# A two-layer decoder trunk on one core: SBUF residues of matmul operands, and the expert's last gate and up blocks as two 512-column slots

## The chip, the cores and the metric

The kernel runs on one core of a Trainium2 chip. The metric is the device time of one execution in microseconds. Before the change it is 1515.24 us, the median of 3 runs (1514.55 to 1516.45).

## The reference

Batch 1, 256 tokens, width 1024, two layers, all in float32. What matters here is which matrices are multiplied:

```python
for l in range(DEPTH):                      # 2 layers
    z = rms_norm(x, mix_norm[l]) @ w_in[l]  # 1024 x 5632: u 512 | q k v 1024 each | two gates 1024 each
    y_a = gelu(s5_branch(u, ...)); y_a = y_a * sigmoid(y_a @ w_glu[l] + b_glu[l])
    y_b = rms_norm(diff_attention(rope(q), rope(k), v, lam), subln[l]) * (1 - lam_init)
    m = sigmoid(g_ssm) * (y_a @ w_proj_ssm[l]) + sigmoid(g_attn) * (y_b @ w_proj_attn[l])
    x = x + m @ w_out[l]
    h = rms_norm(x, ffn_norm[l])
    # layer 0: dense (silu(h @ wg) * (h @ wu)) @ wd, inner width 2816
    # layer 1: the same for 8 experts, top 2 of them per token, weighted
    x = x + (swiglu(h, ...) if l == 0 else moe_swiglu(h, ...))
return rms_norm(x, final_norm)
```

## The kernel before

All weights come as a stream of slots of 128 x 2048 float32 (1 MB), 33 slots for each of three segments (layer 0's mixer, the dense feed-forward, layer 1's mixer) and 33 for each of eight expert rounds. SyncE loads a slot into `w_raw`. ScalarE rounds it into `w_hi` (L562) and VectorE writes the rest into `w_lo` (L568), both as float32r. Every product is then three matmuls (`mm3`, L1758 to L1760): hi x hi, lo (of the stationary operand) x hi, hi x lo (of the moving operand). TensorE's own split operands are `hT` (normed activations, transposed), `yS` and `yB` (the two branches), `actT` (dense activations), `hsT` (the rows of one expert), `eactT` (its activations), `y_slots` and `selectT` (the scatter of an expert's output).

There are two kinds of product. In the U block, the GLU, and the dense gate and up, the weights are stationary (128 x 128 pieces) and the activations move, 256 columns at a time: 48 matmuls a slot. Everywhere else the activations are stationary and the weights move, 512 columns at a time: 24 matmuls a slot in the mixers and in the dense down products (two token tiles), 12 in an expert round. The exception is the expert's last block: the inner width is 2816 = 5 x 512 + 256, so block 5 of gate and of up is 256 wide, one slot each (8 pieces of 256 columns, 24 matmuls).

Segment 1 (dense) runs g0 u0 and then g(j+1) u(j+1) d(j) for j = 0 to 9, then d10. Segments 0 to 2 use three split buffers, slot i in buffer i mod 3. An expert round uses five: three of `w_hi`/`w_lo` and two more, `w_hi_more0/1` and `w_lo_more0/1` (`ROUND_POS`). The splits of ScalarE and VectorE run two slots ahead of TensorE, three in a round. The order on every engine is written out by hand with semaphores; nothing plans it. SyncE also carries small transfers between its loads: twenty for the `s_direct` tile of layer 1 (`shift_direct`, L663) stand between the loads of slots 26 and 27 of segment 1.

The SBUF tiles are laid out one behind the other (`sb`, `room`). For the change the start addresses modulo 512 bytes matter. Slices of weights and activations step by multiples of 512 bytes (128 float32), so every slice of a tile has the tile's residue.

| tiles | residue before |
| --- | --- |
| `hT_hi`, `hT_lo`, `eactT_hi`, `eactT_lo` | 128 |
| `w_hi`, `w_lo`, every slot | 128 |
| `ident`, `identb` / `maskb` | 128 / 384 |
| `hsT`, `actT`, `yS`, `yB`, `y_slots`, `selectT`, `eact_tok`, `x_normed`, `w_hi_more`, `w_lo_more`, q, k, v and the S5 tables | 320 |

Of the kernel before, what the change touches and what calls it, by code (L numbers as in the profile page):

```python
# [9 lines left out]
F32R = mybir.dt.float32r  # L10
# [3 lines left out]
ALU = mybir.AluOpType  # L14
# [29 lines left out]
SLOT = 2048  # L44
SEG = 33
NRAW, NW, AHEAD = 4, 3, 2
RAW_POS = [i % 4 if i < 24 else (i - 24) % 3 for i in range(SEG)]
RAW_USES = [RAW_POS.count(p) for p in range(NRAW)]
GROUP_BLOCK = 512
# [52 lines left out]
ROUND_SLOTS += [("g", 1, 0), ("g", 1, 1), ("u", 1, 0), ("u", 1, 1)]  # L102
for _j in range(2, NB - 1):
    ROUND_SLOTS += [("g", _j, 0), ("d", 2 * _j - 4, 0), ("g", _j, 1), ("d", 2 * _j - 3, 0), ("u", _j, 0), ("u", _j, 1)]
ROUND_SLOTS += [("g", NB - 1, 0), ("u", NB - 1, 0)] + [("d", _m, 0) for _m in range(2 * NB - 6, NJ)]
ROUND_AT = {what: i for i, what in enumerate(ROUND_SLOTS)}
LAST_UP = [ROUND_AT["u", j, 1 if j < NB - 1 else 0] for j in range(NB)]
SCATTERS = [(0, 0, 6), (0, 1, 7), (1, 0, 0), (1, 1, 1)]
NR, RAHEAD = 5, 3
REST_AT, MID_AT, LO_AT = (9, 12), (15, 18), (18, 21)  # L110
# [79 lines left out]
def trunk(nc, t):  # L190
    ctx = ExitStack()
    with ctx:
# [11 lines left out]
        def sb(name, shape, dt=F32):  # L204
            a = here[0]
            here[0] += size(shape, dt)
            return at(name, shape, dt, a)
# [12 lines left out]
        hTh = at("hT_hi", [P, KD, SEQ], F32R, a_hT)  # L220
        hTl = at("hT_lo", [P, KD, SEQ], F32R, a_hT + 8192)
        raw = sb("w_raw", [P, NRAW, SLOT])
        wh = sb("w_hi", [P, NW, SLOT], F32R)
        wl = sb("w_lo", [P, NW, SLOT], F32R)
        ident = sb("ident", [P, P])
        identb = sb("identb", [P, P], BF16)
        maskb = sb("maskb", [P, P], BF16)
# [43 lines left out]
        U4 = sb("uT_lags", [P, PAIRS, BLK])  # L271


        a_q, a_k, a_v = room(8192), room(8192), room(8192)
        a_u, a_yh, a_yl = room(4096), room(4096), room(4096)
        a_tab = room(32768)
# [245 lines left out]
        def raw_of(seg, i):  # L522
            p = (RAW_POS if seg < 3 else ROUND_POS)[i]
            return raw[:, p, :] if p < NRAW else rawx[:, 0, :]

        def split_of(seg, i):

            p = i % NW if seg < 3 else ROUND_POS[i]
            if p < NW:
                return wh[:, p, :], wl[:, p, :]  # L530
            return whx[p - NW][:, 0, :], wlx[p - NW][:, 0, :]

        def landed(seg, i, r=None):
# [539 lines left out]
        def _(dve):  # L1073
# [604 lines left out]
            def dve_round(r, first):  # L1678

                own.r = r  # L1680
                his = [0]

                def hi_taken(name):

                    his[0] += 1
                    assert [w for w in ROUND_TR if w[:2] != "ST"][his[0] - 1] == name
                    dve.wait_ge(s_thi, r * NB + (THI0 + his[0]))
                    return TR0 + ROUND_TR.index(name)

                def act_lo(j):  # L1690
                    t, n = hi_taken(f"act{j}"), block_width(j)
                    V.tensor_tensor(bTl[:, j % 2, 0:n // P].rearrange("p k n -> p (k n)"), bank(4 + t % 2)[:, 0:n],
                                    bTh[:, j % 2, 0:n // P].rearrange("p k n -> p (k n)").bitcast(F32),
                                    ALU.subtract).then_inc(s_trf[t % 2], 1)

                for i in range(SEG):
                    if i == 3:
                        scattered(r)
                        for q in range(NT):
                            n = TR0 + ROUND_TR.index(f"ST{q}")  # L1700
                            dve.wait_ge(s_tr, r * R_TR + (n + 1))
                            V.tensor_copy(ST[:, q * P:(q + 1) * P], bank(4 + n % 2)[:, 0:P]).then_inc(s_trf[n % 2], 1)
                    if i in (29, 31):
                        act_lo(4 + (i - 29) // 2)
                    if i in (30, 31):
                        dve.wait_ge(s_hsh, r * 2 + (2 + i - 29))
                        hs_lo(i - 30)
                    round_split(dve_split, dve, i, r)
                    if first and i in REST_AT:
                        q = REST_AT.index(i)  # L1710
                        dve.wait_ge(s_hsw, 2)
                        dve.wait_ge(s_xh, q + 1)
                        V.tensor_tensor(xn[:, q, :], xn[:, q, :], xnh[:, q, :], ALU.subtract).then_inc(s_xr, 1)
                    if first and i in LO_AT:
                        q = LO_AT.index(i)
                        dve.wait_ge(s_xm, q + 1)
                        V.tensor_tensor(xnl[:, q, :], xn[:, q, :], xnm[:, q, :], ALU.subtract).then_inc(s_xl, 1)
                    if i == 4:
                        dve.wait_ge(s_scatv, r * 4 + 4)
                        own.do(V.tensor_copy(gcol[:, :], gateR[:, :, bass.ds(r, 1)].rearrange("p t o -> p (t o)")))  # L1720
                    if i in (7, 13, 19, 25):
                        act_lo((i - 7) // 6)
                    if i == SEG // 2:

                        own.do(V.tensor_copy(pcol[:, :], placeR[:, :, bass.ds(r + 1, 1)].rearrange("p t o -> p (t o)")))
                        select()
                    if i in LAST_UP[:5] or i == 28:
                        j = LAST_UP.index(i) if i in LAST_UP else 5
                        n = block_width(j)
                        dve.wait_ge(s_sg, r * NB + (GU0 + j + 1))  # L1730
                        if j == 5:
                            dve.wait_ge(s_tr, r * R_TR + (TR0 + ROUND_TR.index("act4") + 1))
                        V.tensor_tensor(moe_act[:, 0:n], moe_sg[:, 0:n], bank(3 + 4 * (j % 2))[:, 0:n], ALU.mult).then_inc(s_act, 1)

                for c in range(2):
                    dve.wait_ge(s_ysh, r * 2 + (c + 1))
                    V.tensor_tensor(ysl[:, c * 512:(c + 1) * 512], bank(c), ysh[:, c * 512:(c + 1) * 512].bitcast(F32),
                                    ALU.subtract).then_inc(s_ysl, 1)
# [14 lines left out]
        def _(pe):  # L1753
# [344 lines left out]
            with pe.Fori(0, rounds) as r:  # L2098

                def up(i):  # L2100

                    kind, j, h = ROUND_SLOTS[i]
                    n = block_width(j)
                    if kind == "g" and h == 0:
                        if j == 0:
                            pe.wait_ge(s_hsf, r * 2 + 1)
                        elif j == 1:
                            pe.wait_ge(s_scatv, r * 4 + 2)
                        else:
                            pe.wait_ge(s_act, r * NB + (GU0 + j - 1))  # L2110
# [3 lines left out]
                    nk = SLOT // n  # L2114
                    H, L = parts(3, i, nk)
                    for k in range(nk):
                        m = mm3(bank(2 + 4 * (j % 2) + "gu".index(kind))[:, 0:n], hsh[:, nk * h + k, :], hsl[:, nk * h + k, :],
                                H[:, k, :], L[:, k, :], start=(h == 0 and k == 0), stop=(nk * h + k == KD - 1))
                    m.then_inc(s_gu if i in LAST_UP else s_used, 1)

# [94 lines left out]
def round_slot(gate, up, down, what):  # L2215
    kind, j, h = what
    if kind == "d":
        return slot_of(down, 2 * j, 2, 0, D)
    n = block_width(j)
    return slot_of(gate if kind == "g" else up, SLOT // n * h, SLOT // n, 512 * j, n)  # L2220


def weight_stream(a):
# [41 lines left out]
```

## Time and profile before

| what | value |
| --- | --- |
| median of three runs | 1515.24 us |
| the profiled execution, first to last instruction (the only time the page has for it) | 1514.5 us |
| TensorE busy | 1475.5 us, 97%, 9071 matmuls |
| VectorE / ScalarE busy | 1226.9 us (81%) / 888.7 us (59%) |
| one expert round | 98.25 us, eight of them |
| 256-column products with `w_hi` or `w_lo` stationary and `hT` moving | 416 in each of L1758, L1759, L1760 |
| 512-column products with `hsT` stationary, `w` / `w_more` moving | 384 / 256 in each of the three lines |
| mean granted TensorE clock over the span | 0.993 |

TensorE takes a new matmul before the last one has ended, so a matmul's duration (0.28 us for 256 columns, about 0.39 for 512) is longer than the time from its start to the next start. The latter is what a stretch costs. It is read from the timeline: the difference of two start times, divided by the number of matmuls between them.

### The profile page before, as it was taken

To read this page: it belongs to the slowest core of one execution; us is meant where nothing else is said; L and a number is where in the kernel's file an instruction comes from. 1 tells how busy PE (TensorE), PEld (TensorE's weight loads), DVE (VectorE), ACT (ScalarE), POOL (GpSimd) and SP (SyncE) were. 2 spreads that over 40 slices of the span, in tenths; PEclk is the share of its full clock that TensorE was granted. 3 is DMA by queue.
4 is the path that set the end of the run, shared out by engine and by line. 5 is a ranking of instruction groups with operands and counts; after the bars stand their busy time and mean duration, and the time that the engine had idled before them with its cause. 6 is when DMAs were issued, how large, how long until landed. Compare 5 with 4: busy or idle time off the path is not lost.

```text
span 1514.5 us, 23848 instructions
## 1 busy us (share of the span) xinstructions
PE 1475.5 (97%) x9071; PEld 1247.5 (82%) x9071; DVE 1226.9 (81%) x1307; ACT 888.7 (59%) x887; POOL 74.1 (5%) x123
## 2 busy tenths in 40 slices
PE   7999999999999999998999999999999999999997
PEld 6788878999988888887888888888888888888886
DVE  7897786665456787867999989888888898988987
ACT  5244654443344346634677677767677767767775
POOL 2900100000000000101000000000000000000000
PEclk9899999999999999999999999999999999999999
DMA  6444444554355443353999989999999998998994
GB/s 247 156 139 149 151 154 180 209 175 180 92 204 198 167 150 108 142 197 146 366 360 347 378 335 353 359 345 361 346 346 370 341 357 339 350 374 334 351 360 166
DMA packets 76931, 393.09 MB, mean 260 GB/s; under 512 B 28225, under 2 KB 28353, under 8 KB 30018
## 3 DMA queue, kind: packets, MB, share of 16 engines
q1 hardware_dynamic: 75392, 391.28, 68.9%
q10 hardware_dynamic: 1474, 0.91, 0.2%
q8 instruction: 44, 0.72, 0.2%
q14 instruction: 21, 0.17, 0.0%
HBM read 388.36 MB, written 1.05 MB: 257 GB/s over the span
## 4 chain that ended last, share of the span: by engine, by line
PE 88%; DVE 6%; ACT 2%; issue 2%; SPq 1%; DMA 1%; POOL 0%; DVEq 0%; ACTq 0%; POOLq 0%
PE psum L1758 26%; PE psum L1760 26%; PE psum L1759 26%; PE psum L1774 3%; PE psum L2072 1%; DVE w_lo L568 1%; ACT w_hi L562 1%; SPq L663 1%; PE psum L1825 1%; PE psum L1870 1%; PE psum L2095 1%; PE psum L1807 1%; PE psum L2096 1%; PE psum L1800 0%; DMA w_raw<-in_stream 0%
## 5 line engine op out<-in xcount | busy, mean ns | idle before, releaser
L568 DVE TENSOR_TENSOR w_lo<-w_raw,w_hi 128x2048 fp32r<-128x2048 f32 x270 | 613.7, 2290 | 146.6 <-ACT w_hi L562 145.5
L562 ACT ACTIVATE w_hi<-w_raw 128x2048 fp32r<-128x2048 f32 x270 | 513.8, 1914 | 247.2 <-PE psum L1760 221.6
L1758 PE MATMUL psum<-w_hi,hsT_hi 128*128 128x512 f32 (+1 forms) x512 | 188.7, 369 | 2.1 <-issue 2.1
L1759 PE MATMUL psum<-w_hi,hsT_lo 128*128 128x512 f32 (+1 forms) x512 | 186.9, 365 | 0.0
L1760 PE MATMUL psum<-w_lo,hsT_hi 128*128 128x512 f32 (+1 forms) x512 | 186.7, 365 | 0.0
L1758 PE MATMUL psum<-w_hi,hT_hi 128*128 128x512 f32 x384 | 156.4, 407 | 4.8 <-DVE w_lo L568 4.6
L1760 PE MATMUL psum<-w_lo,hT_hi 128*128 128x512 f32 x384 | 151.3, 394 | 0.0
L1759 PE MATMUL psum<-w_hi,hT_lo 128*128 128x512 f32 x384 | 151.2, 394 | 0.0
L568 DVE TENSOR_TENSOR w_lo_more<-w_raw,w_hi_more 128x2048 fp32r<-128x2048 f32 x56 | 128.1, 2287 | 12.3 <-ACT w_hi_more L562 12.3
L1758 PE MATMUL psum<-hT_hi,w_hi 128*128 128x256 f32 x416 | 119.1, 286 | 4.9 <-DVE act_ff L1508 3.1
L1759 PE MATMUL psum<-hT_hi,w_lo 128*128 128x256 f32 x416 | 118.5, 285 | 0.0
L1760 PE MATMUL psum<-hT_lo,w_hi 128*128 128x256 f32 x416 | 118.4, 285 | 0.0
L562 ACT ACTIVATE w_hi_more<-w_raw 128x2048 fp32r<-128x2048 f32 x56 | 107.0, 1910 | 10.2 <-DMA w_raw<-in_stream 6.5
L1758 PEld LDWEIGHTS psum<-w_hi,hsT_hi 128*128 128x128 f32 x512 | 96.6, 189 | 18.2 <-issue 2.3
L1760 PEld LDWEIGHTS psum<-w_lo,hsT_hi 128*128 128x128 f32 x512 | 96.6, 189 | 16.8
L1759 PEld LDWEIGHTS psum<-w_hi,hsT_lo 128*128 128x128 f32 x512 | 96.7, 189 | 15.6
L1758 PE MATMUL psum<-w_hi_more,hsT_hi 128*128 128x512 f32 x256 | 102.4, 400 | 0.0
L1760 PE MATMUL psum<-w_lo_more,hsT_hi 128*128 128x512 f32 x256 | 100.2, 391 | 0.0
L1759 PE MATMUL psum<-w_hi_more,hsT_lo 128*128 128x512 f32 x256 | 99.6, 389 | 0.0
L1059 ACT ACTIVATE esilu_g<-psum 128x512 f32<-128x512 f32 (+1 forms) x48 | 27.1, 564 | 113.0 <-PE psum L1760 113.0
L568 DVE TENSOR_TENSOR w_lo_more<-w_raw_more,w_hi_more 128x2048 fp32r<-128x2048 f32 x40 | 91.4, 2284 | 0.1
L1758 PEld LDWEIGHTS psum<-w_hi,hT_hi 128*128 128x128 f32 x384 | 73.3, 191 | 20.5 <-DVE w_lo L568 5.2
(400 smaller groups left out, 2796.6 us busy)
## 6 DMA issues: line engine op xcount, KB each, us to landing
w_raw<-in_stream SPq DMA_DIRECT2D x326, 1024.0 KB, 5.6
w_raw_more<-in_stream SPq DMA_DIRECT2D x40, 1024.0 KB, 6.7
gain_row<-in_gain_rows SPq DMA_DIRECT2D x3, 512.0 KB
x_tok<-in_x SPq DMA_DIRECT2D x1, 1024.0 KB, 4.9
uT_lags<-uT_by_lag SPq DMA_DIRECT2D x64, 16.0 KB, 1.9
zT_by_lag<-uT_lags SPq DMA_DIRECT2D x64, 16.0 KB, 1.8
out_trunk<-out_tok SPq DMA_DIRECT2D x2, 512.0 KB, 2.6
s_direct<-s_direct_lags SPq DMA_DIRECT2D x40, 16.0 KB, 2.0
```

The source lines that it names most:

```text
L562: nc.scalar.activation(split_of(seg, i)[0], raw_of(seg, i), ACT.Copy).then_inc(s_hi, 1)
L568: nc.vector.tensor_tensor(l_, raw_of(seg, i), h.bitcast(F32), ALU.subtract).then_inc(s_lo, 1)
L663: sp.dma_start(Tm[rows(g, d), :, LAGS - 1 - d + e, :], TS[rows(g, e), :, :]).then_inc(s_tm, 16)
L1059: nc.scalar.activation(moe_sg[:, 0:n], bank(2 + 4 * (j % 2))[:, 0:n], ACT.Silu).then_inc(s_sg, 1)
L1758: mm(out, lh, rh, start=start, stop=False)
L1759: mm(out, ll, rh, start=False, stop=False)
L1760: return mm(out, lh, rl, start=False, stop=stop)
L1774: i = nc.tensor.transpose(dst[:, k * P:(k + 1) * P], s, ident[:, :])
L1807: mm(b[r, p * GCH:(p + 1) * GCH], Bl[l][r, c, p, :, :].rearrange("p d n -> p (d n)"), E[r, p, 0, :], start=(p == 0 and c == 0), stop=False)
L1825: mm(bank(2 + c)[:, off:off + n], qT[c * 64:(c + 1) * 64, h, q * P:(q + 1) * P], kT[c * 64:(c + 1) * 64, h, 0:n], start=(q == 1), stop=False)
L1870: i = mm(bank(6)[r, c * 256 + k * BLK:c * 256 + (k + 1) * BLK], Bt[r, c, p, :], U4[r, p, :], start=(k == 0 and c == 0), stop=(k == 3 and c ...
L2072: i = mm(bank(2 + g)[:, kk * P:(kk + 1) * P], part[:, q, k * P:(k + 1) * P], S[:, q, :], start=(part is xnh and kk == 0 and q == 0), stop= ...
```

## The change

Three things. First, padding: a pad after `w_hi` and one ahead of `a_q` bring `w_lo` and all the tiles from `a_q` on to the residue of `hT`, 128. Second, the three split buffers get 48 elements (192 bytes) at their end, and where a slot's weights are the stationary operand, the slot is put 192 bytes further, at residue 320. This holds for the dense gate and up slots (all but the first up slot, i = 1) and for the first slot of each mixer segment (the first half of the U block). The buffers are also renumbered, `(p + 2) % NW`. Third, the last gate and up blocks, 256 columns each, are laid side by side in the stream, so that the two slots are the upper and the lower half of the 1024 rows with 512 columns, gate in columns 0 to 255 and up in 256 to 511. Both accumulate in one bank, and VectorE takes up from its second half. The number of slots, their bytes and the waits stay.

```diff
+LEAD = 48
-ROUND_SLOTS += [("g", NB - 1, 0), ("u", NB - 1, 0)] + [("d", _m, 0) for _m in range(2 * NB - 6, NJ)]
+ROUND_SLOTS += [("gu", NB - 1, 0), ("gu", NB - 1, 1)] + [("d", _m, 0) for _m in range(2 * NB - 6, NJ)]
-LAST_UP = [ROUND_AT["u", j, 1 if j < NB - 1 else 0] for j in range(NB)]
+LAST_UP = [ROUND_AT["u" if j < NB - 1 else "gu", j, 1] for j in range(NB)]
...
-        wh = sb("w_hi", [P, NW, SLOT], F32R)
-        wl = sb("w_lo", [P, NW, SLOT], F32R)
+        wh = sb("w_hi", [P, NW * SLOT + LEAD], F32R)
+        here[0] += (a_hT - here[0]) % 512
+        wl = sb("w_lo", [P, NW * SLOT + LEAD], F32R)
...
+        here[0] += (a_hT - here[0]) % 512
         a_q, a_k, a_v = room(8192), room(8192), room(8192)
...
+        def stationary(seg, i):
+
+            if seg == 1:
+                return i % NW != 1 and FFN_SLOTS[i][0] != "d"
+            return seg != 3 and i == 0
+
         def split_of(seg, i):
 
             p = i % NW if seg < 3 else ROUND_POS[i]
             if p < NW:
-                return wh[:, p, :], wl[:, p, :]
+                a = (p + 2) % NW * SLOT + (LEAD if stationary(seg, i) else 0)
+                return wh[:, a:a + SLOT], wl[:, a:a + SLOT]
...
-                        V.tensor_tensor(moe_act[:, 0:n], moe_sg[:, 0:n], bank(3 + 4 * (j % 2))[:, 0:n], ALU.mult).then_inc(s_act, 1)
+                        ups = bank(3 + 4 * (j % 2)) if j < NB - 1 else bank(2 + 4 * (j % 2))[:, n:2 * n]
+                        V.tensor_tensor(moe_act[:, 0:n], moe_sg[:, 0:n], ups[:, 0:n], ALU.mult).then_inc(s_act, 1)
...
-                    n = block_width(j)
-                    if kind == "g" and h == 0:
+                    n = 512
+                    if kind[0] == "g" and h == 0:
...
-                        m = mm3(bank(2 + 4 * (j % 2) + "gu".index(kind))[:, 0:n], hsh[:, nk * h + k, :], hsl[:, nk * h + k, :],
+                        m = mm3(bank(2 + 4 * (j % 2) + (kind == "u"))[:, 0:n], hsh[:, nk * h + k, :], hsl[:, nk * h + k, :],
...
+    if kind == "gu":
+        last = np.concatenate([w[:, 512 * j:512 * j + block_width(j)] for w in (gate, up)], 1)
+        return slot_of(last, 4 * h, 4, 0, 512)
+    return slot_of(gate if kind == "g" else up, 4 * h, 4, 512 * j, 512)
```

The residues after it: 128 for `hT`, `eactT`, `hsT`, `actT`, `yS`, `yB`, `y_slots`, `selectT`, `eact_tok`, `x_normed`, both `w_more` pairs and every `w` slot whose weights move; 320 for the `w` slots with the lead and for `ident` and `identb`; 64 for `maskb`.

On TensorE the instructions change in one place, the last gate and up blocks of a round. Before, the end of the slot ahead, and the boundary from the gate slot to the up slot (`hsT` are the expert's rows, stationary; `act_ready` frees the banks):

```order
L1760 MATMUL psum<-w_lo,hsT_hi 128x512
L2113 REGISTER_ALU [waits act_ready]
L1758 MATMUL psum<-w_hi,hsT_hi 128x256 [waits w_lo_ready]
L1759 MATMUL psum<-w_hi,hsT_lo 128x256
L1760 MATMUL psum<-w_lo,hsT_hi 128x256
...
L1760 MATMUL psum<-w_lo,hsT_hi 128x256
L2113 REGISTER_ALU
L1758 MATMUL psum<-w_hi,hsT_hi 128x256 [waits w_lo_ready]
L1759 MATMUL psum<-w_hi,hsT_lo 128x256
```

The same place now, on TensorE again (line numbers of the changed kernel are 11 higher here):

```order
L1771 MATMUL psum<-w_lo,hsT_hi 128x512
L2124 REGISTER_ALU [waits act_ready]
L1769 MATMUL psum<-w_hi,hsT_hi 128x512 [waits w_lo_ready]
L1770 MATMUL psum<-w_hi,hsT_lo 128x512
L1771 MATMUL psum<-w_lo,hsT_hi 128x512
...
L1771 MATMUL psum<-w_lo,hsT_hi 128x512
L2124 REGISTER_ALU
L1769 MATMUL psum<-w_hi,hsT_hi 128x512 [waits w_lo_ready]
L1770 MATMUL psum<-w_hi,hsT_lo 128x512
```

Each of the two slots had 24 matmuls of 256 columns and has 12 of 512 now; the waits stand in the same places. ScalarE, VectorE, GpSimd and SyncE have the same instructions in the same order.

## Rows read from the trace of the kernel before

**Rows 1.** The page, shares of the chain that ended last.

```profile
PE 88%; DVE 6%; ACT 2%; issue 2%; SPq 1%; DMA 1%; POOL 0%; DVEq 0%; ACTq 0%; POOLq 0%
```

**Rows 2.** By stretch: length, busy PE PEld DVE ACT POOL, PEclk, DMA share, GB/s.

```profile
288.00:422.00 134.00, 132.73 (x1121) 123.53 (x1119) 78.94 (x81) 52.48 (x43) 0.00 (x0) 1.00 0.47 165
910.32:1008.57 98.25, 98.25 (x501) 81.55 (x500) 86.91 (x60) 69.48 (x49) 0.00 (x0) 1.00 0.92 353
```

**Rows 3.** SyncE queue's waits in one round, 910.32 to 1008.57: total, times, longest.

```profile
SPq L620 <- DVE w_lo L568: 54.6, 21, 5.4
SPq L620 <- DVE w_lo_more L568: 22.8, 11, 4.7
```

**Rows 4.** Timeline of TensorE (start us, duration us, ...), a dense up slot.

```profile
299.76 0.28 PE L1758 MATMUL psum<-hT_hi,w_hi 128*128 128x256 f32 x1
...
304.08 0.40 PE L1758 MATMUL psum<-w_hi,actT_hi 128*128 128x512 f32 x1
```

**Rows 5.** The same view, an expert's last gate and up block.

```profile
985.79 0.28 PE L1758 MATMUL psum<-w_hi,hsT_hi 128*128 128x256 f32 x1
...
991.12 0.28 PE L1760 MATMUL psum<-w_lo,hsT_hi 128*128 128x256 f32 x1
```

**Rows 6.** The same view, layer 1's GLU slot.

```profile
607.72 0.28 PE L1758 MATMUL psum<-yS_hi,w_hi 128*128 128x256 f32 x1
...
609.64 0.28 PE L1760 MATMUL psum<-yS_lo,w_hi 128*128 128x256 f32 x1
```

**Rows 7.** The same view, layer 1's mixer, behind a group of transposes.

```profile
506.34 0.39 PE L1759 MATMUL psum<-w_hi,hT_lo 128*128 128x512 f32 x1
...
508.18 0.39 PE L1758 MATMUL psum<-w_hi,hT_hi 128*128 128x512 f32 x1
...
513.85 0.39 PE L1759 MATMUL psum<-w_hi,hT_lo 128*128 128x512 f32 x1
```

**Rows 8.** The same view, an expert slot in the extra buffers.

```profile
923.50 0.39 PE L1758 MATMUL psum<-w_hi_more,hsT_hi 128*128 128x512 f32 x1
...
925.99 0.39 PE L1760 MATMUL psum<-w_lo_more,hsT_hi 128*128 128x512 f32 x1
```

**Rows 9.** The same view, an expert slot, transposes, and the next slot.

```profile
928.53 0.39 PE L1759 MATMUL psum<-w_hi,hsT_lo 128*128 128x512 f32 x1
...
931.50 0.40 PE L1760 MATMUL psum<-w_lo,hsT_hi 128*128 128x512 f32 x1
931.73 0.60 PE L1774 MATMUL psum<-ident,eact_tok 128*128 128x128 f32 x4
932.09 0.47 PE L1758 MATMUL psum<-w_hi,hsT_hi 128*128 128x512 f32 x1
932.40 0.39 PE L1759 MATMUL psum<-w_hi,hsT_lo 128*128 128x512 f32 x1
```

**Rows 10.** The same view, a round's last down slot and the next round's start.

```profile
1005.77 0.39 PE L1758 MATMUL psum<-w_hi_more,eactT_hi 128*128 128x512 f32 x1
...
1008.57 0.40 PE L1758 MATMUL psum<-w_hi,hsT_hi 128*128 128x512 f32 x1
```

**Rows 11.** Timeline of VectorE and TensorE, dense, the gate that follows an activation.

```profile
308.49 0.68 DVE L1508 TENSOR_TENSOR act_ff<-silu_g,psum 128x512 f32<-128x512 f32 x1
...
309.59 0.28 PE L1758 MATMUL psum<-hT_hi,w_hi 128*128 128x256 f32 x1
```

**Rows 12.** The chain of waits, 385 to 430 us: start us, us, what.

```profile
398.07 0.39 ACT s_direct_lags L862
...
412.75 5.27 DMA w_raw<-in_stream
...
422.94 0.38 PE psum L1758
```

**Rows 13.** Timeline of TensorE, start of the gather in a round.

```profile
997.22 0.62 PE L2072 MATMUL psum<-select,x_normed_hi 128*128 128x128 bf16 x8
997.68 0.61 PE L2072 MATMUL psum<-select,x_normed_mid 128*128 128x128 bf16 x8
```

More of the change, by code:

```diff
@@ L2218, in round_slot @@
         return slot_of(down, 2 * j, 2, 0, D)
-    n = block_width(j)
-    return slot_of(gate if kind == "g" else up, SLOT // n * h, SLOT // n, 512 * j, n)
+    if kind == "gu":
+        last = np.concatenate([w[:, 512 * j:512 * j + block_width(j)] for w in (gate, up)], 1)
+        return slot_of(last, 4 * h, 4, 0, 512)
+    return slot_of(gate if kind == "g" else up, 4 * h, 4, 512 * j, 512)
 def weight_stream(a):
```

## The prediction

> **What bounds the kernel now.** Read the chain of waits first: 88% of it is TensorE, so the sum of TensorE's work is nearly the time [rows 1]. Then the busy times by stretch: an expert round (98.25 us, eight of them) has TensorE busy all of its 98.25 us at a granted clock of 1.00 (the 2.4 GHz level), and the dense feed-forward stretch 132.73 of 134.00 us, also at 1.00 [rows 2]. VectorE (86.9) and ScalarE (69.5) have room in a round, and DMA is busy for 0.92 of it. The SyncE queue waits 54.6 + 22.8 = 77 of 98 us for VectorE to hand back raw buffers, so the transfers wait for the compute and not the other way round [rows 3]. What is left is the time from one matmul's start to the next. The durations in the groups (0.28 and 0.39 us) overlap and hide it; the timeline's start times, divided by the number of products, give it.
>
> **The spacing and the addresses.** I write a|b for the residue modulo 512 of the moving operand and of the stationary operand that is loaded for the next product while the first one streams.
> - 256 columns, 128|128 (dense gate and up): 299.76 to 304.08 us is 36 products, 120.0 ns each [rows 4].
> - 256 columns, 128|320 (the expert's last block): 985.79 to 991.12 is 47 steps, 113.4 ns [rows 5].
> - 256 columns, 320|128 with the weights stationary (GLU): 607.72 to 609.64 is 17 steps, 113 ns, though its later half runs near 118 [rows 6]. So it is not the weights' being stationary that costs the dense products their 6.6 ns.
> - 512 columns, 128|128 (mixer): after a break 506.34 to 508.18, 8 steps of 230 ns, then 508.18 to 513.85, 25 steps of 226.8 ns [rows 7]. It settles at 226.8, and settling costs 8 x 3.2 = 0.026 us.
> - 512 columns, 320|320 (expert slots in the extra buffers): 923.50 to 925.99, 11 steps of 226.4 ns [rows 8]. So equality counts, not the residue itself.
> - 512 columns, 128|320: 928.53 to 931.50, 13 steps of 228.5 ns [rows 9]. 512 columns, 320|128: 1005.77 to 1008.57, 12 steps of 233.3 ns [rows 10].
>
> So 256-column products want unequal residues (113.4 against 120.0) and 512-column ones equal residues (226.6 against 228.5 to 233.3), and the change gives each what it wants.
>
> **Dense gate and up.** 22 slots of 48 products; all but the first up slot get a stationary operand 192 bytes further: 21 x 48 = 1008 products go from 128|128 to 128|320. 1008 x (120.0 - 113.4) = 6.65 us. Is TensorE alone the limit there? The next gate waits for the activation, which ends at 308.49 + 0.68 = 309.17, and the gate starts at 309.59 when the down slot is through [rows 11]: 0.4 us of slack, and since that chain starts with the end of the up slot, only the down slot (24 products, 0.05 us faster) eats into it. It holds. One stretch does not: ScalarE's copy at 398.07 starts twenty small SyncE transfers that run until 412.75, behind them the weights' own load, and at its end TensorE restarts at 422.94 after sitting idle [rows 12]. That chain is in fixed time; the TensorE work beside it, two slots of 48 and two down slots, gets shorter by 96 x 6.6 = 0.63 and 48 x 1.5 = 0.07 us, and the wait grows by as much: 0.7 us lost. Left 5.95 us.
>
> **Rounds.** A round's 98.25 us less the last block (48 x 0.1134 = 5.44), the gather (48 products; eight take 0.46, together 2.7 [rows 13]), the 22 transposes (four take 0.36 [rows 9]) and two selects, together 2.1, and eight first products after a transpose or a wait that take 0.31 instead of 0.23 [rows 9], 0.7 us, leaves 87.3 us for 380 products of 512 columns: 229.8 ns. After the change all of them stand at 128|128: the hs operands, the transposed activations, y_slots and the extra weight buffers all move from residue 320 to 128. I take 226.7 ns, and 0.026 us for settling at eight places: 380 x 3.1 = 1.18, less 0.21, is 0.97 us a round, 7.8 us for eight. The down slots that sit in the extra buffers gain the most, 6.6 ns a product [rows 10].
>
> **The last block as two slots of 512 columns.** It takes away 24 products and their 24 weight loads a round: 24 x 226.7 = 5.44 us against 48 x 113.4 = 5.44. Nothing. The instruction orders show the same two waits for w_lo and the same one for the activation; the gate half was ready 2.7 us before the up half, but SiLU waited for the end of the up slot before too. Both halves now stand in one bank; no row shows what reading one bank in turn costs, and the room that ScalarE and VectorE have in a round (29 and 11 us) covers it. Bounds: 24 x 233.3 would be 0.16 us a round more; should half the weight loads free another 6.6 ns a product, 0.16 us less; so 1.3 us either way in all.
>
> **The small rest.** 264 dense down products and 288 of the two projections go from 128|320 to 128|128, 228.5 to 226.7: 1.0 us. Layer 1's first U slot gains 48 x 6.6 = 0.3; layer 0's is hidden, TensorE waits for setup behind it. The 96 GLU products lose, from 320|128 to 128|128: between 0.2 and 0.65 us, I take 0.5. The fp32 transposes (ident moves from 128 to 320, their source from 320 to 128) are not shown at that pair; 176 of them in the rounds and about as many before. The nearest rows are the 256-column ones, up to 5 ns dearer at 320|128 than at 128|320 [rows 5, 6], so half that for 128 columns: up to 0.9 us worse or, if the order is the other way round there, better; I take 0.
>
> **The sum.** 5.95 + 7.8 + 0 + 1.0 + 0.3 - 0.5 = 14.5 us. The profiled execution spans 1514.5 us, the median is 0.7 above it: 1500.0 and so 1500.7 us.
>
> **The Trainium skill against it.** The rows say that a product's spacing depends on two addresses [rows 4, 5]. "TensorE: Matmul & The Clock Gate", section "Step-by-step: what each phase is for", says of the two read ports that "Loading the next tile's weights doesn't steal SBUF read bandwidth from the running matmul". By that rule the residues change nothing and the sum is 0; by the rows it is 14.5. It is the first rival.
>
> **The rivals.**
> 1. The spacing follows the place in the program and not the addresses: 1515.2 us. For it: no two of my rows differ in the address alone. Against it: five kinds of place sort by the pair of residues, and buffers at 320|320 agree with 128|128 to 0.4 ns [rows 7, 8]. 3%.
> 2. The rounds are held by something else as soon as TensorE is faster, DMA at 0.92 of its time the nearest: only dense and small terms stay, 1508.5 us. Against it: DMA would go to 0.93, with SyncE waiting 77 us a round [rows 2, 3]. 5%.
> 3. Half of the round's gain: the 512-column products do not settle between the slots and average 228.3, the middle between 226.7 and the 229.8 of today: 1504.5 us. 12%.
> 4. The dense products stay at 120 (their stationary slices step through k and halves, the last block's through k alone): 1507 us. 4%.
> 5. Slower: equal residues are the dear pair for 512 columns as they are for 256, 2 x 120.0 = 240 ns. Then 404 products of each round cost 10.2 ns more, 33.0 us, the 552 of the small rest 11.5 more, 6.3 us, less 5.75 for dense, U and GLU: 1549 us. It decides as soon as they exceed 231 ns, where it eats those 5.75. Against it stand [rows 7, 8], which show 226.4 to 226.8 at equal residues. 1%.
>
> **How the numbers follow.** The forecast has 75%: its own range is 1498.5 to 1503 (the settling gone, 1.7 us; the unknown transposes and the bank, 2 us, either way). Reaching to rival 3 on the upper side and a little beyond gives 1498 to 1506, which leaves rivals 1, 2, 4 and 5 (13%) and some of the forecast's own tails outside. About 0.2% (3 us) is what a measurement of this kernel can tell from no change. Faster by more than that: the forecast and rivals 2, 3 and 4, 96% less 1 for what I don't see; within: rival 1, 3%; slower: rival 5 and that 1, 2%.
>
> **What would show it.** Dense gate and up starts 113.4 ns apart, except in the first up slot (120). Steady 512-column stretches at 226.7 everywhere in a round, and a round of 97.3 us with TensorE still busy throughout; DMA share 0.93. The restart after the small transfers 0.7 us more idle than before. GLU at 120. The last block still 5.44 us. Wrong, if a round stays above 97.9 us, if TensorE waits for w_lo within one, or if the dense spacing is not below 116.

## The result and the profile after

| | before | after |
| --- | --- | --- |
| median | 1515.48 us (4 runs) | 1506.91 us (1506.29 to 1508.38, 4 runs) |
| ratio of the runs | | 0.9943, 95% interval 0.9932 to 0.9955 |
| the profiled execution's span | 1514.5 us | 1504.9 us |
| one expert round | 98.25 us | 97.27 us |
| dense stretch, from gate 0's first product to up 10's last (start to start) | 188.58 us | 186.98 us |

The kernel is 8.6 us faster, where 14.5 were forecast; 1506.91 us lies 0.9 us above the range. The two profiled executions differ by 9.6 us: dense stretch 1.60, the rounds with their tail 8.19, everything else together -0.2. The changed kernel's profiled execution took 1506.65 us by the metric and spans 1504.9; by the same 1.75 us the profiled one of before, 1514.5, was about 0.8 us above its median (an estimate), so the profiles show more than the medians do.

The busy times by stretch of the changed kernel (length, then PE, PEld, DVE, ACT, POOL busy, granted clock, DMA share, GB/s): the dense stretch up to gate 9, a piece of it, and a round.

```profile
288.00:420.91 132.91, 132.91 (x1117) 123.58 (x1116) 78.91 (x81) 51.10 (x42) 0.00 (x0) 0.97 0.47 167
395.00:402.00 7.00, 7.00 (x48) 5.28 (x46) 2.02 (x2) 0.38 (x1) 0.00 (x0) 0.51 0.10 11
906.53:1003.80 97.27, 97.27 (x478) 80.60 (x477) 86.97 (x60) 69.26 (x49) 0.00 (x0) 1.00 0.93 353
```

The round is 0.98 us shorter than in [rows 2], TensorE is busy for all of it at a granted clock of 1.00, and DMA went from 0.92 to 0.93. The window of the dense stretch ends 0.94 us before gate 9 both times. The 1.3 us in which TensorE stood idle within it (2.2 us up to gate 9) are gone, but the granted clock is 0.97, because between 395 and 402 us it is half of full speed (1.2 GHz). SyncE's waits in the round are the old ones, 52.9 + 23.5 us against 54.6 + 22.8 [rows 3]:

```profile
SPq L630 <- DVE w_lo L578: 52.9, 21, 4.7
SPq L630 <- DVE w_lo_more L578: 23.5, 11, 4.6
```

TensorE's timeline (start us, duration us) in a dense up slot after the change. From 298.00 to 302.59 there are 39 steps: 117.7 ns each, where the forecast had 113.4 and [rows 4] had 120.0.

```profile
298.00 0.28 PE L1769 MATMUL psum<-hT_hi,w_hi 128*128 128x256 f32 x1
...
302.59 0.28 PE L1769 MATMUL psum<-hT_hi,w_hi 128*128 128x256 f32 x1
```

The same view, the expert's last gate and up block, now two slots of 512 columns, and the slot in the extra buffers behind it. 981.17 to 986.61 is 24 steps of 226.7 ns, 5.44 us, as long as the 48 products of [rows 5].

```profile
981.17 0.39 PE L1769 MATMUL psum<-w_hi,hsT_hi 128*128 128x512 f32 x1
...
986.61 0.39 PE L1769 MATMUL psum<-w_hi_more,eactT_hi 128*128 128x512 f32 x1
```

A round's last down slot: 1001.05 to 1003.77 is 12 steps of 226.7 ns, where [rows 10] show 233.3.

```profile
1001.05 0.39 PE L1769 MATMUL psum<-w_hi_more,eactT_hi 128*128 128x512 f32 x1
...
1003.77 0.39 PE L1769 MATMUL psum<-w_hi,hsT_hi 128*128 128x512 f32 x1
```

Layer 1's GLU slot: 605.99 to 608.26 is 19 steps of 119.5 ns (120 settled), against 113 in [rows 6]; and a group of four transposes, 0.35 us as in [rows 9].

```profile
605.99 0.28 PE L1771 MATMUL psum<-yS_lo,w_hi 128*128 128x256 f32 x1
...
608.26 0.28 PE L1769 MATMUL psum<-yS_hi,w_hi 128*128 128x256 f32 x1
...
927.59 0.60 PE L1785 MATMUL psum<-ident,eact_tok 128*128 128x128 f32 x4
927.94 0.48 PE L1769 MATMUL psum<-w_hi,hsT_hi 128*128 128x512 f32 x1
```

The chain of waits around gate 9 (start us, us, what). In [rows 12] it ran through SyncE, a DMA and an activation, and TensorE restarted at 422.94. Now the view keeps to TensorE, past the first product of gate 9 at 421.85.

```profile
396.46 0.93 PE psum L1821 x4
397.39 0.72 PE psum L1769
398.12 0.43 PE psum L1770
...
401.96 0.31 PE psum L1770
402.27 0.23 PE psum L1771
...
421.74 0.23 PE psum L1771
421.97 0.27 PE psum L1769
```

The products from 398 to 402 us take 0.43 us each instead of 0.23: the half clock. Behind the chain's start they fill time in which TensorE had idled. Ahead of it they cost: the four setup products whose end releases ScalarE's copy, the start of the fixed-time chain of [rows 12], take 0.93 us there, and 0.50 before the change.

The timeline at gate 9 shows that TensorE's work and the chain ended almost together. The activation ends at 421.11 + 0.68 = 421.79 us, and the gate's first weight load is put down to it; behind the down slot alone the gate would have started 0.04 us earlier.

```profile
421.11 0.68 DVE L1518 TENSOR_TENSOR act_ff<-silu_g,psum 128x512 f32<-128x512 f32 x1
...
421.58 0.39 PE L1771 MATMUL psum<-w_lo,actT_hi 128*128 128x512 f32 x1
421.85 0.19 PEld L1769 LDWEIGHTS psum<-hT_hi,w_hi 128*128 128x128 f32 x1 [0.30 <-DVE act_ff L1518]
```

### The profile page after: what moved, and what is told of

Same layout as the page of the kernel before. It is cut to its first block, busy times and chain, and to the rows that moved or that the text cites. A ratio compares the mean times of both kernels' runs of the same rounds, so it can differ in the third digit from the quotient of the medians.

```text
span 1504.9 us, 23464 instructions
## 1 busy us (share of the span) xinstructions
PE 1468.6 (98%) x8879; PEld 1240.1 (82%) x8879; DVE 1227.1 (82%) x1307; ACT 889.0 (59%) x887; POOL 74.2 (5%) x123
## 4 chain that ended last, share of the span: by engine, by line
PE 88%; DVE 7%; ACT 2%; issue 1%; DMA 0%; POOL 0%; ACTq 0%; POOLq 0%; DVEq 0%
PE psum L1769 27%; PE psum L1771 26%; PE psum L1770 26%; PE psum L1785 3%; DVE w_lo L578 2%; PE psum L2083 1%; ACT w_hi L572 1%; PE psum L1836 1%; PE psum L1881 1%; PE psum L1818 1%; PE psum L2106 0%; PE psum L2107 0%; ACT prob L969 0%; PE psum L1811 0%; DMA columns<-in_columns 0%
## 5 line engine op out<-in xcount | busy, mean ns | idle before, releaser
L1769 PE MATMUL psum<-w_hi,hsT_hi 128*128 128x512 f32 x448 | 176.0, 393 | 2.0 <-issue 2.0
L1771 PE MATMUL psum<-w_lo,hsT_hi 128*128 128x512 f32 x448 | 174.5, 390 | 0.0
L1770 PE MATMUL psum<-w_hi,hsT_lo 128*128 128x512 f32 x448 | 174.3, 389 | 0.0
L1769 PE MATMUL psum<-hT_hi,w_hi 128*128 128x256 f32 x416 | 118.3, 284 | 2.7 <-DVE hT_lo L1282 1.8
L1771 PE MATMUL psum<-hT_lo,w_hi 128*128 128x256 f32 x416 | 117.6, 283 | 0.0
L1770 PE MATMUL psum<-hT_hi,w_lo 128*128 128x256 f32 x416 | 117.4, 282 | 0.0
L1769 PEld LDWEIGHTS psum<-w_hi,hsT_hi 128*128 128x128 f32 x448 | 84.1, 188 | 19.0 <-issue 2.2
L1771 PEld LDWEIGHTS psum<-w_lo,hsT_hi 128*128 128x128 f32 x448 | 84.1, 188 | 17.8
L1770 PEld LDWEIGHTS psum<-w_hi,hsT_lo 128*128 128x128 f32 x448 | 84.2, 188 | 17.0
```

Of the source, the lines that this page charges most:

```text
L1769: mm(out, lh, rh, start=start, stop=False)
L1770: mm(out, ll, rh, start=False, stop=False)
L1771: return mm(out, lh, rl, start=False, stop=stop)
```

## The experiments

Distances are from the moving operand's row to the slice that is loaded meanwhile, in bytes modulo 512. "Settled" spacings are means over the last 24 products of a slot, from start times in the trace. A time without a range is that of a single run. Beside the first four experiments the kernel before took 1517.18 us, beside the others 1515.8 to 1516.0 in the median.

**Distances, first map.** One distance for each dense block, and seven other distances in seven slots of a round.

```diff
-LEAD = 48
+LEAD = 112
+DENSE_LEADS = [112, 104, 96, 80, 64, 56, 48, 32, 24, 16, 8]
+ROUND_LEADS = {0: 16, 5: 32, 10: 64, 15: 80, 20: 96, 25: 112, 29: 48}
```

> The changed kernel with another distance in each dense block: the gate and up slots of block j are put 448, 416, 384, 320, 256, 224, 192, 128, 96, 64, 32 bytes further for j = 0 to 10 (192 everywhere in the changed kernel), and in a round the moving weights of slots 0, 5, 10, 15, 20, 25, 29 are put 64, 128, 256, 320, 384, 448, 192 bytes further. Theory A (the spacing of a 256-column product is a function of the distance modulo 512): each block settles at its own spacing, 118 at 192 bytes, 120 near 0, and some distance, most likely around 256 or 320, at 113 or below; 512-column slots differ by distance too, 229 to 233 at 320 (192 back), 226.7 at none. Theory B (any unequal distance gives the same and something else makes 118): all dense blocks at 118 whatever the distance.

1512.12 us. 256 columns, settled, in ns (distance 0 is the first up slot, each other distance one block): distance 0 120.0, 32 118.3, 64 117.8, 96 117.3, 128 120.0, 192 117.8, 224 116.7, 256 120.0, 320 117.8, 384 120.0, 416 120.0, 448 117.8. 512 columns in the rounds, means over all steps of the slot but the one behind a break, seven rounds: distance 0 227.8, or 226.7 once settled, 64 233.2, 128 232.6, 192 230.3, 256 226.7, 320 233.5, 384 232.7, 448 230.3. Two slots of one round, distance 384 and distance 256:

```profile
827.10 0.40 PE L1779 MATMUL psum<-w_hi,hsT_hi 128*128 128x512 f32 x1
...
829.89 0.39 PE L1779 MATMUL psum<-w_hi,hsT_hi 128*128 128x512 f32 x1
...
841.28 0.39 PE L1779 MATMUL psum<-w_hi,hsT_hi 128*128 128x512 f32 x1
...
844.00 0.39 PE L1779 MATMUL psum<-w_hi,eactT_hi 128*128 128x512 f32 x1
```

From 841.28 to 844.00 there are 12 steps of 226.7 ns; the slot at 384 ran from 827.10 to 829.89, 12 steps of 232.5. So for 512 columns the distance moves the spacing, with its best at 0 and 256. Distances 256 bytes apart give nearly the same: 233.2 and 233.5 at 64 and 320, 232.6 and 232.7 at 128 and 384, 230.3 twice at 192 and 448. But the distance alone doesn't fix the number. In the kernel before, at 128|320, the first three slots of each round from the second on keep another spacing than the slot of [rows 9] (228.5 ns): from 1009.04 to 1016.74 there are 33 steps of 233.3 ns.

```profile
1009.04 0.40 PE L1760 MATMUL psum<-w_lo,hsT_hi 128*128 128x512 f32 x1
...
1016.74 0.40 PE L1760 MATMUL psum<-w_lo,hsT_hi 128*128 128x512 f32 x1
```

For 256 columns none of the twelve distances gave 113.4, the distance of 192 neither, though the last block of before had it.

**The last block's loop order in the dense slots.** If the step pattern of the stationary slices made the difference, this gives 113.4.

```diff
-                            for c in range(2):
-                                cs = slice(c * P, (c + 1) * P)
-                                for k in range(KD):
+                            for k in range(KD):
+                                for c in range(2):
+                                    cs = slice(c * P, (c + 1) * P)
```

> The changed kernel with the loops of a dense gate or up slot exchanged: the k piece outside, the column half inside, so the order of the stationary pieces and the run of moving pieces are another, with the same addresses overall. Theory A (distance modulo 512 alone): 118 ns as now. Theory C (the sequence of whole addresses matters, beyond modulo 512): another spacing, 113.4 if the last block's sequence was what made it cheap. About 1007 us times nothing else changes: 1506 to 1507 us if it stays, 1502 if it becomes 113.4.

1506.79 us: 117.8 in 20 slots, but 113.3 in gate 0 (the first up slot, which has no lead, stays at 120.0). The order isn't the cause. Yet block 0 shows that 113.3 exists at these addresses.

**Small products ahead of a gate.** These are bfloat16 products of `maskb` with `identb`, 128 columns, whose results nobody reads; eight of them move the gate's start by 0.43 us. The numbers are for blocks 0 to 10.

```diff
+                            if j and not n:
+                                idle_products([0, 1, 2, 3, 4, 5, 6, 8, 10, 12, 16][j])
```

> The changed kernel with 1, 2, 3, 4, 5, 6, 8, 10, 12, 16 small bfloat16 products put in front of the gate slot of dense blocks 1 to 10, each 0.056 us, 3.8 us in all. Theory D (two steady rhythms exist at this distance, 113.4 and 118, and the one taken depends on how the slot is entered): some blocks settle at 113.4 and others at 118. Theories A and C: all stay at 118.

1506.12 us. Gate and up of block 7 (8 small products) and block 10 (16) settle at 113.3, as does gate 0; all others at 117.8. The timeline shows block 7 (381.06 to 386.96, 52 steps of 113.5 ns) and block 8 (404.18 to 409.95, 49 steps of 117.8 ns), with the same addresses.

```profile
380.32 0.62 PE L1791 MATMUL psum<-maskb,identb 128*128 128x128 bf16 x8
380.75 0.36 PE L1769 MATMUL psum<-hT_hi,w_hi 128*128 128x256 f32 x1
...
381.06 0.28 PE L1771 MATMUL psum<-hT_lo,w_hi 128*128 128x256 f32 x1
...
386.96 0.28 PE L1769 MATMUL psum<-hT_hi,w_hi 128*128 128x256 f32 x1
...
403.31 0.73 PE L1791 MATMUL psum<-maskb,identb 128*128 128x128 bf16 x10
403.85 0.36 PE L1769 MATMUL psum<-hT_hi,w_hi 128*128 128x256 f32 x1
...
404.18 0.28 PE L1771 MATMUL psum<-hT_lo,w_hi 128*128 128x256 f32 x1
...
409.95 0.28 PE L1769 MATMUL psum<-hT_hi,w_hi 128*128 128x256 f32 x1
```

**The distance modulo 1024.**

```diff
-        here[0] += (a_hT - here[0]) % 512
+        here[0] += (a_hT - here[0]) % 1024
         wl = sb("w_lo", [P, NW * SLOT + LEAD], F32R)
```

> The changed kernel with w_lo 512 bytes further on, so that w_hi and w_lo have the same residue modulo 1024 as in the kernel before (it was 512 apart in the changed one). Theory C in its simplest form (modulo 1024 counts and the high and low weights should agree in it): dense spacing 113.4 instead of 118 and 1502 us. Theories A and D: 118 and no change, 1506 to 1507 us.

1506.29 us, 117.8 in all the slots with a lead. The position of `w_lo` modulo 1024 isn't the cause.

**More entries.** The same edit with other counts.

```diff
+                                idle_products([0, 8, 8, 8, 16, 16, 16, 12, 20, 7, 9][j])
```

> The changed kernel with 8, 8, 8, 16, 16, 16, 12, 20, 7, 9 small products in front of the gate slots of dense blocks 1 to 10. If the number of small products sets the rhythm, all blocks with 8 and 16 settle at 113.4 (blocks 7 and 10 did, with 8 and 16). If it is chance at the start, or depends on where the slot's instruction falls in time, some do and some don't.

1510.85 us. Blocks 2 to 5 (8, 8, 16, 16) settle at 113.3 in gate and up; blocks 7 to 10 (12, 20, 7, 9) at 117.8, and so do blocks 1 and 6 (8 and 16). These two don't stand behind a down slot: ahead of block 1 TensorE idles for 0.85 us behind the first up slot, ahead of block 6 stand 64 setup products. The small products cost more than they bring: eight and the refill behind them add 0.51 us to a block that then saves 0.43.

**One short product instead of eight.**

```diff
+                            if not n:
+                                for w_ in [[], [64], [16], [32], [48], [64], [32], [96], [128], [8], [112]][j]:
+                                    mm(bank(7)[:, 0:w_], identb[:, :], maskb[:, 0:w_], start=True, stop=True)
```

> One small bf16 product stands ahead of each dense gate block from the second on, of 64, 16, 32, 48, 64, 32, 96, 128, 8 and 112 columns (blocks 1 to 10); in the counts tried before, 8 or 16 products of 128 columns were followed by 113.3 in all six blocks that did not start after an idle stretch, and 1 to 7, 9, 10, 12 or 20 of them by 117.8 in all. Theory (the phase in which a block falls in sets one of two lasting rhythms at the same addresses): some widths give 113.3 in gate and up alike, others 117.8, and a block that hits costs 0.43 us less, while the product itself costs 0.1 to 0.2 us. Rival (the long run of small products empties or fills something, and one product is too short for that): 117.8 in all ten blocks. Time 1505 to 1509 in either case.

1505.70 us. All ten blocks at 117.8; gate 0, without such a product, at 113.3.

The second set of widths, 16, 24, 40, 56, 80, 96, 4, 88, 120 and 104:

> The same with 16, 24, 40, 56, 80, 96, 4, 88, 120 and 104 columns. As for the other set of widths: by the theory a few of these give 113.3 in gate and up, by the rival none does. If the same width (16, 96) gives different spacings in the two kernels, the width alone does not set the rhythm.

1507.29 us, 117.8 in all eleven gates. Twenty blocks with sixteen widths and no hit: one short product isn't enough, and to that extent the rival has it. The theory of the phase isn't refuted by this, though. The width hardly moves the gate: from the last down product to the gate's first there are 0.27 us in every block behind a down slot that doesn't wait, whether the product has 4 columns or 128, and 0.23 without one. So the sixteen widths tried a single shift, of 0.04 us.

**Distances, second map.** `DENSE_LEADS = [120, 88, 72, 60, 58, 56, 54, 52, 50, 44, 40]`, the rounds as in the changed kernel.

> The changed kernel with ten more distances from the moving row to the next stationary slice in the dense gate and up products, block 0 to block 10: 480, 352, 288, 240, 232, 224, 216, 208, 200, 176 and 160 bytes (modulo 512). The first map had 113.3 to 118.3 at the distances 32 to 96, 192, 224, 320 and 448 and 120.0 at 0, 128, 256, 384 and 416. If the distance modulo 512 sets the spacing smoothly, the values run between those of the neighbours: 208 and 216 between 117.8 and 116.7, 240 from 116.7 to 120, 160 and 176 between 120 and 117.8; 224 gives 116.7 once more. If the spacing is a matter of the rhythm into which a block falls, neighbours 8 bytes apart jump between 113.3, 116.7, 117.8 and 120 without order, and 224 need not give 116.7 again. Time 1505 to 1512.

1506.02 us. Settled: 480 116.7, 352 118.6, 288 118.3, 240 117.4, 232 118.3, 224 116.7, 216 120.0, 208 116.7, 200 120.0, 176 118.1, 160 120.0. Neighbours 8 bytes apart jump between 116.7 and 120.0, which is the second reading, but 224 repeats. So do distances 256 bytes apart over the two maps: 32 and 288, 64 and 320, 128 and 384, 160 and 416, 0 and 256, 192 and 448, 224 and 480 agree within 0.1 ns; only 96 and 352 don't (117.3 and 118.6). That speaks for the address, even though most values come from one block each and the next experiments show that a block can have another one.

**A lead of 224 bytes, timed.** `LEAD = 56`.

> The lead is 56 elements (224 bytes) in place of 48 (192 bytes). The one look at it gave 116.67 ns where 192 bytes gave 117.8: 1.1 x 1008 = 1.1 us less, 1505.5 to 1506. If the spacing falls back on 117.8, 1506.5 to 1507, no change to the changed kernel.

1506.52 us (1505.28 to 1508.04), ratio 0.9945 [0.9931, 0.9958]. The trace has 116.7 in most slots and 117.8 in blocks 0 (its gate), 6 and 9, so at 224 too there are two values. A gain of 1 us can't be told from none here: it doesn't beat the changed kernel.

**No lead.** Both conditions of `stationary` return False.

```diff
-                return i % NW != 1 and FFN_SLOTS[i][0] != "d"
-            return seg != 3 and i == 0
+                return False
+            return False
```

> The changed kernel without the 192-byte lead: all weights' slots at residue 128, so dense gate and up are at 128|128 again. If the lead brings what the profile of the changed kernel shows (117.8 against 120.0 ns on 1008 products, 2.2 us, less some tenths in the stretch with the fixed chain), this is 2 us slower than the changed kernel: 1508.5 to 1509. If the lead brings nothing, 1507.

1507.50 us (1506.52 to 1509.02), ratio 0.9939 [0.9922, 0.9956]. All dense gate and up slots at 120.0, the rounds at 97.27 us. The timing can't separate it from the changed kernel, the trace can: the lead is worth 2.2 ns a product, 2.2 us at most.

**The merged slots alone**, on the kernel before (the change's edits of `ROUND_SLOTS`, `LAST_UP`, the bank and the stream, no padding and no lead).

> The kernel before with only the last gate and up blocks as two slots of 512 columns, no padding. My sum had nothing for it: 1515 to 1516, within 0.1% of before. A gain from the halved weight loads would be up to 1.3 us, a loss from the 128|320 spacing of 512-column products (229 to 233 ns against 2 x 113.4) 0.4 to 1.3 us.

1515.62 us (1514.79 to 1516.29), ratio 0.9998 [0.9988, 1.0007]. Nothing, and a round of it is still 98.31 us:

```profile
810.20:908.51 98.31, 98.31 (x478) 80.62 (x476) 87.06 (x60) 69.47 (x49) 0.00 (x0) 1.00 0.93 353
```

**The padding and the lead without the merged slots.**

```diff
-ROUND_SLOTS += [("gu", NB - 1, 0), ("gu", NB - 1, 1)] + [("d", _m, 0) for _m in range(2 * NB - 6, NJ)]
+ROUND_SLOTS += [("g", NB - 1, 0), ("u", NB - 1, 0)] + [("d", _m, 0) for _m in range(2 * NB - 6, NJ)]
```

> The pads and leads of the changed kernel, with the expert's last gate and up blocks as they were before: four products of 256 columns a token tile in place of two of 512. Theory: the whole gain of the rounds is the padding (before, the products of 512 columns stand at 229.0 to 232.9 with distances of 0, 192 and 320; after at 227.3 with 0), and the merged slots are worth nothing. Then the last block stays 94 products at 113.3, or at 120 if the padding puts its moving rows at a distance of 0 like the dense ones of before (48 x 2 x 6.7 = 0.64 us a round, 5.1 us in all). The first reading gives the changed kernel's time within 1 us (1506 to 1508), the second 1511 to 1513. Rival: the merged slots themselves carry the gain, 1514 to 1515.

1510.57 us (1507.23 to 1511.42), ratio 0.9961 [0.9948, 0.9975]: between the two. A round takes 97.61 us, and the last block says why: 886.31 to 891.94 is 47 steps of 119.8 ns.

```profile
811.66:909.27 97.61, 97.61 (x502) 81.83 (x501) 86.90 (x60) 69.37 (x49) 0.00 (x0) 1.00 0.94 354
```

```profile
886.31 0.28 PE L1768 MATMUL psum<-w_hi,hsT_hi 128*128 128x256 f32 x1
...
891.94 0.28 PE L1770 MATMUL psum<-w_lo,hsT_hi 128*128 128x256 f32 x1
```

With the padding these 48 products (the expectation counted them twice) stand at 128|128, and cost 48 x 6.5 = 0.31 us a round more, 2.5 us in all; by the rounds' lengths it is 97.61 - 97.27 = 0.34, or 2.7 us. The merged slots buy that back, since 512 columns are at their best there. The other products of the round gain 0.95 us by the padding alone.

**Dense activations at 320.** The down slots get back the distance of 192.

```diff
-        aTh = at("actT_hi", [P, 2, 2, SEQ], F32R, a_u)
-        aTl = at("actT_lo", [P, 2, 2, SEQ], F32R, a_yh)
+        aTh = at("actT_hi", [P, 2, 2, SEQ], F32R, a_u + 192)
+        aTl = at("actT_lo", [P, 2, 2, SEQ], F32R, a_yh + 192)
```

> The changed kernel with the dense activations (actT) 192 bytes further, so that the down products run at 128|320 as before the change and the gate slot behind them is entered out of such products, as the last block was in the kernel before. Theory D (two steady rhythms, chosen at the entry): the gate and up slots settle at 113.4 instead of 117.8, about 4.4 us less, the downs cost 0.5 us more, some tenths vanish in the fixed chain: 1503 to 1504. Theory E (the rhythm at entry is chance): some blocks at 113.4, 1504 to 1507. If the downs before it don't matter: 1507.4.

1506.66 us (1504.41 to 1508.05), ratio 0.9928 [0.9911, 0.9946]. The steps between down products average 229.3 ns instead of 227.7 (229.0 before the change): 0.4 us over 264 products, below what the timing can tell. Block 7 fell into 113.3 without any small product.

**The changed kernel once more.**

> The changed kernel once more, in the same sitting as the two others, so that they are compared on one chip: 0.9943 of before, 1506.5 to 1508. Its profile shows whether the two low-clock stretches (395.2 us, 6.8 us long, and 466.9 us, 3.4 us long) come again: if they belong to the kernel's short products at these places they do, within a few us; if they are chance, they lie elsewhere or are gone. And whether gate block 0 is at 117.8 again or at the 113.3 that two variants with the same addresses showed there.

1506.88 us (1505.84 to 1508.37), ratio 0.9943 [0.9930, 0.9957]. 117.8 in all the slots with a lead. The low-clock stretch near 396 us came again, half as long; the one at 466.9 didn't:

```profile
395.00:402.00 7.00, 7.00 (x64) 5.38 (x63) 2.37 (x2) 0.38 (x1) 0.00 (x0) 0.76 0.10 12
```

## Why the prediction was right and where it failed

- **The rounds were right.** A round is 0.98 us shorter where 0.97 was forecast, with TensorE still the limit, and every slot that doesn't follow a break stands at 226.7. With the first round and the tail it is 8.2 us against 7.8, but 0.7 us of that is the clock: the profiled execution of before had 3.4 us at 1.2 GHz in its first round, at 712.5 us, and the one after had none. The executions with the changed rounds take 793.9 to 794.0 us from there to the end without such a stretch and 794.6 to 794.7 with one, so like for like the gain is 802.2 - 794.65 = 7.5 us. It comes from the padding, in the 512-column products: 0.95 us a round, less the 0.3 that it costs the last block unless the slots are merged (97.27 us without the lead, 97.61 without the merged slots, 98.31 with the merged slots alone). The renumbering of the buffers wasn't tried apart from the padding. The first map shows the cause by address alone: 226.7 at a distance of 0 and 256, 230 to 233.5 at six others, in slots of one round. It refutes rivals 1 and 5, and the round's length refutes rivals 2 and 3.
- **Dense gate and up was mis-sized.** This is the step that failed: "1008 x (120.0 - 113.4) = 6.65 us". The products went from 120.0 to 117.8, so the term is 1008 x 2.2 = 2.2 us, 4.4 less, and 117.8 is also above the 116 that the prediction named as its sign of being wrong. I took the 113.4 of another place for the spacing that the residue pair 128|320 has; but that pair has two lasting rhythms, 113.3 and 117.8, as blocks 7 and 8 of the run with small products show. A hint was in view, at the mirrored pair 320|128: the later half of the GLU slot "runs near 118", I wrote, and used the slot only to excuse the weights' being stationary. It is steady, 611.99 to 613.99 us, 17 steps of 117.6 ns, while the first half in [rows 6] is at 113:

```profile
611.99 0.28 PE L1758 MATMUL psum<-yS_hi,w_hi 128*128 128x256 f32 x1
...
613.99 0.28 PE L1760 MATMUL psum<-yS_lo,w_hi 128*128 128x256 f32 x1
```

- **Rival 4** (the dense products stay at 120) is refuted too. That its time, 1507, is the one that came is chance: the lead moves the spacing by a third of what I counted, and 120.0 comes back without it. Its cause, the order of the slices, is refuted by the loop order run.
- **What chooses the rhythm** stays open. It isn't the addresses alone, since blocks of one kernel with equal addresses show both; nor the loop order, nor the position modulo 1024. Directly behind a down slot, eight or sixteen small products gave 113.3 in six blocks of six. The other counts tried, ten from 1 to 12 and 20, never did (12 blocks, ten of them behind a down slot), and one short product didn't either (20 blocks, 16 behind a down slot). Without any small product it came in one block of 48 behind a down slot at this distance, block 7 of the run with the activations at 320. In gate 0 it came in 3 executions of 10, and two of the three had no edit ahead of it: there the same instructions gave 113.3 once and 117.8 another time. So chance plays a part, and each count was run once only. Why eight, no run shows.
- **The fixed-time chain** still released gate 9, as forecast, but only just, and the wait didn't grow as the prediction had it: TensorE idles 2.2 us there before, 0.0 in the profile after and 1.2 in the kernel run once more. From gate 0 to gate 6 the profiled execution saves 1.28 us, about what 11 slots of 48 products at 2.2 ns and the down slots give. From gate 6 to gate 9 it saves nothing, 58.1 us against 58.0. The forecast's loss there, put at 117.8, would be 96 x 2.2 = 0.2 us. The rest is the low clock from 395.2 us, ahead of the chain's start: the setup products up to ScalarE's copy took 5.40 us (392.03 to 397.43) and 4.43 before (393.64 to 398.07). The run with the second set of widths had no low stretch there and took 57.1 us from gate 6 to gate 9, short products included. So up to 1 us of the shortfall in the profile is the clock, and not the change. Nor is the chain's time fixed to such tenths: from the copy's start to the activation's end it took 24.8 us before and 24.1 to 24.9 in the other executions.
- **The last block** cost nothing, as forecast, 5.44 us each. But "nothing" holds for the sum only: with the padding in place the merge is worth 2.5 to 2.7 us by the traces, because padding alone moves these products from the good pair to the bad one. The forecast compared before with after, and missed that one edit pays for the other.
- **The small rest** was forecast at 0.8 us, of which 0.5 are down slots within the dense stretch. Of those 0.35 came (steps of 227.7 from 229.0 ns). Outside it the profiled execution shows -0.2 where 0.3 was forecast. Its pieces: the projections' steps went down by 1.5 to 1.7 ns, 0.45 us in all, the GLU's up by 3.5, 0.3 us, the transposes stayed, and layer 1's first U slot went from 120.0 to 117.8 and not to 113.4. But the stretch between the dense one and the rounds took 259.4 to 262.7 us in the executions with the padding and 259.7 and 260.9 in the two without. A piece of some tenths can't be seen in that.

The prediction's rival 1 had beside it a sentence of the Trainium skill, in "TensorE: Matmul & The Clock Gate", section "Step-by-step: what each phase is for", that loading the next weights doesn't take read bandwidth from the running matmul; read as the prediction read it, the sum would have been 0. The runs contradict that reading: moving nothing but a weight slot modulo 512 bytes changes 226.7 to 233.5 ns. Whether it is bandwidth or something else that collides, no run here shows.

## What to carry to other kernels

Where TensorE sets the time, divide start-to-start times by the number of products, place by place: equal instructions that differ by 3% point to the addresses, or to how the stretch was entered. For float32r here the distance from the moving row to the next stationary slice wants to be 0 or 256 modulo 512 bytes at 512 columns, and neither of the two at 256 columns (120.0 ns, as at 128 and 384); change one buffer's base and look again. When a layout is changed for one kind of product, look which other kind loses by it. Before a spacing seen in one place is multiplied by a thousand products in another, look whether the same pair of addresses, or the mirrored one, shows a second value anywhere: then the term has two ends and the range must hold both.

## What the hardware showed unexpectedly

- A lasting rhythm can differ at equal addresses: 113.3 or 117.8 ns for whole gate and up slots, 96 products, with a down slot between two blocks to end it; and 233.3 or 228.5 ns for 512 columns at 128|320 within one round of the kernel before. In the changed kernel's rounds, at a distance of 0, every slot that isn't behind a break stands at 226.7.
- With 256 columns the spacing jumps with 8 bytes (116.7 at 208, 120.0 at 216, 116.7 at 224, 118.3 at 232, one block each but 224) and comes again at nearly all distances 256 bytes apart.
- The clock fell to the 1.2 GHz level for 3.4 or 6.8 us near 395 us in 11 of the 16 profiles, behind setup products on 64 rows, most of them of 16 columns, without idle time between them, and not in the one of before. In three of the other five it fell near 421 us, at the end of 2.0 to 2.4 us in which TensorE idled. In 12 of the 16, the one of before among them, it fell between 709 and 715 us, behind 2 us of idle time that all 16 have; that stretch made the rounds 0.7 us longer. Where TensorE sets the time all along, 3.4 us at half the clock cost 1.7 us, by estimate. The two profiles of the changed kernel itself differ in it (6.8 and 3.4 us near 395, and one more at 466.9 in the first).
